# Reordering PE's small solve products in the RWKV-7 heads of a two-layer kernel

## The chip, the cores and the metric

The kernel runs on one core of a Trainium2 chip. The metric is the device time of one execution in microseconds (us), the median of the runs shown. Five engines run side by side and meet only at semaphores: TensorE (PE, with its weight loads as PEld), VectorE (DVE), ScalarE (ACT), GpSimd (POOL) and SyncE (SP, which here only starts DMAs).

## The reference

Two layers run one after the other on 256 tokens of width 2048. The first is a gated mixer with a feed-forward part, the second a hybrid layer with banded attention, an RWKV-7 recurrence and memory cross attention. The change lies in the second layer, where one head of attention and two heads of the recurrence are computed together:

```python
def rwkv7_scan(r, decay, k, v, a_vec, b_vec):
    def step(state, inp):
        r_t, w_t, k_t, v_t, a_t, b_t = inp
        sa = jnp.einsum('bhij,bhj->bhi', state, a_t)
        state = state * w_t[:, :, None, :] + sa[..., None] * b_t[:, :, None, :] + v_t[..., None] * k_t[:, :, None, :]
        return state, jnp.einsum('bhij,bhj->bhi', state, r_t)
    ...

def hybrid_layer(x, mem, norm_g, w_in, ...):
    h = rms_norm(x, norm_g)
    proj = h @ w_in
    (aq, ak, av, az, br, bk, bv, bz, bwd, bad, cq, cz, ga, gb, gc) = jnp.split(proj, offsets, axis=-1)
    ya = chunked_band_attention(aq, ak, av, a_rel_bias) * jax.nn.silu(az)
    yb = rwkv7_time_mix(br, bk, bv, bwd, bad, ...).astype(x.dtype) * jax.nn.silu(bz)
    ...
    return x + merged @ w_o
```

## The kernel before

All large products run in float32 made of three passes: a weight unit of 512 KB (4 x 128 rows by 256 columns) lands in `raw`, ACT rounds it to `w_hi`, DVE makes the rest `w_lo = raw - w_hi` (L1391), and PE multiplies hi by hi, hi by lo and lo by hi. One unit is 24 matmuls of 128x128 weights by 256 columns. Units go through a ring of four. ACT splits unit k+4 as soon as PE has finished unit k, and DVE follows ACT.

The recurrence runs in chunks of 64 tokens, four chunks, two 64-wide heads at once on the upper and lower 64 partitions. Inside a chunk a triangular system is solved by products of 64x64 matrices. A *burst* here is one or two such products for all four chunks and both heads. The function `corners` interleaves two products so that the four 64x64 corners of the array take turns, which makes 32 matmuls.

`late(units)` is written once for each engine and holds the solve of one pair of heads. It runs eight times: seven times in a loop over `heads` (the 16 projection units of the next pair of heads are mixed in) and once with the first 16 units of another projection. `units(k)` means one thing on each engine: PE multiplies unit k (with a second argument, only one half of it, 12 matmuls), ACT makes `w_hi` and DVE `w_lo` of the unit that follows four later in the ring. Every engine works strictly in the order written, and nothing else sets the order. On PE the bursts that matter here are called so in what follows:

- **A**: `No*Q` and `Q*No`, then `Q*At` and `Q*AkV` (64 matmuls)
- **B**: `b2*b1` and `b1*b2`, whose results ACT copies to `N` and `Nt`
- **C**: `N*F` and `Nt*N`, then **T**: three transposes of the softmax weights `prb` (L742)
- **D**: `b3*F` (16 matmuls); DVE adds it to `F`
- **E**: `Y*F` and `F*Kt`, whose results ACT copies to `b2` and `b1`
- after that `state(0)`, `output(0)`, `solve(1)`, `state(1)` and so on: the walk from chunk to chunk, between half units. DVE carries the state `S` and the term `SA` in it (`state`, `solved`).

The order on PE is: unit 3, A, first half of unit 4, B, second half of unit 4, C, T, unit 5, D, unit 6, E, first half of unit 7, `state(0)`. On ACT, `keep(name, bank)` copies a product out of PSUM and tells PE. On DVE, `prepare()` after `units(5)` is `keys_of`, nine operations for the keys of the next pair of heads, and it stands ahead of the first update of `S`. `step` and `to_pe` on DVE both mark an operation done; only `to_pe` is counted by PE's `from_dve()`.

Of the kernel before, what the change touches and what calls it, by code (L numbers as in the profile page):

```python
# [36 lines left out]
HEADS_A = 8  # L37
# [130 lines left out]
def build(nc, a):  # L168
    out_ap = a["out"]
    with ExitStack() as ctx:  # L170
# [91 lines left out]
        bd = {}  # L262
# [123 lines left out]
        def b64(bank):  # L386
            return banks[bank][:, 0:NCH * CHUNK].rearrange("p (c t) -> p c t", c=NCH)
# [35 lines left out]
        def _(pe):  # L423
            n = Counts(pe)
# [71 lines left out]
            for q, (tab, src) in enumerate(((0, f_sum), (1, f_bwd))):  # L496
                for f in range(2):
                    for c in range(2):
# [3 lines left out]
                        for k in range(2):  # L502
                            m = mm(banks[b][:, 0:384], dft[:, tab, k, f * P:(f + 1) * P],
                                   src[:, k, c * 384:(c + 1) * 384], k == 0, k == 1)
# [6 lines left out]
            for c in range(2):  # L511
                for half in range(2):
                    b = 3 + 2 * c + half
                    for j in range(3):
                        m = pe.transpose(banks[b][:, j * P:(j + 1) * P], z1[:, 3 * half + j, c * P:(c + 1) * P],
                                         con_("ident"))
# [4 lines left out]
            for i, (f, c) in enumerate(((0, 0), (0, 1), (1, 0), (1, 1))):  # L521
                if i >= 2:
                    from_dve()
                for part in range(2):
                    b = 3 + 2 * (i % 2) + part
                    for k in range(2):
                        m = mm(banks[b][:, 0:384], dft[:, part, k, f * P:(f + 1) * P],
                               zt[:, k, c * 384:(c + 1) * 384], k == 0, k == 1)
# [3 lines left out]
            for j in range(HY):  # L532
                o = banks[3 + j // 2][:, (j % 2) * T:(j % 2 + 1) * T]
                for i, (src, tab, k) in enumerate(((k_re, 2, 0), (k_re, 2, 1), (k_im, 3, 0), (k_im, 3, 1))):
                    m = mm(o, src[:, k, j * P:(j + 1) * P], dft[:, tab, k, :], i == 0, i == 3)
# [4 lines left out]
            for j in range(HY):  # L540
                m = mm(banks[6][:, 0:T], con_("ones"), gv[:, j, :], j == 0, j == HY - 1)
# [3 lines left out]
            for j in range(HY):  # L545
                m = mm(banks[7][:, 0:T], con_("ones"), gsq[:, j, :], j == 0, j == HY - 1)
# [3 lines left out]
            for e in range(HY):  # L550
                for c in range(2):
                    i = 2 * c + e % 2
                    m = pe.transpose(banks[3 + e // 2][:, i * P:(i + 1) * P], gv[:, e, c * P:(c + 1) * P],
                                     con_("ident"))
# [5 lines left out]
            for e in range(HY):  # L560
                for c in range(2):
                    o = banks[3 + e // 2][:, (e % 2) * T + c * P:(e % 2) * T + (c + 1) * P]
                    m = mm(o, gvt[:, c, e * P:(e + 1) * P], ws[:, e, :])
# [3 lines left out]
            for g in range(4):  # L567
                m = mm(banks[6 + g // 2][:, (g % 2) * T:(g % 2 + 1) * T], pw[:, g, :], pool_d[:, g, :])
# [16 lines left out]
            for half in range(2):  # L585
# [5 lines left out]
                for q in range(4):  # L591
# [5 lines left out]
                    for u in range(11):  # L597
# [6 lines left out]
                        for kk in range(2):  # L604
                            for t in range(4):
# [5 lines left out]
                                m = mm(o, wl, rh, False, u == 10 and kk == 1 and t % 2 == 1)  # L611
# [7 lines left out]
            def product(out, lhs, rhs):  # L619

                return lambda hs, c: mm(out[hs, c, :], lhs(hs, c), rhs(hs, c))
# [7 lines left out]
            def corners(*products):  # L629

                n_, last = len(products), [None] * len(products)
                for j in range(n_):
                    turns = [(j, 0), ((j + 1) % n_, 1)]
                    for c in range(NCH):
                        for i, h in (turns if j == 0 else turns[::-1]):
                            last[i] = products[i](HALVES[h], c)
                return last
# [37 lines left out]
            def late(units):  # L675
# [3 lines left out]
                m = {name: of(t) for name, t in bd.items()}  # L679
# [3 lines left out]
                p, q = corners(product(b4(3), m["b"], both), product(b4(5), m["k"], both))  # L683
                p.then_inc(psum_for_dve, 1)
                q.then_inc(psum_for_dve, 1)
                p, q = corners(product(b64(4), a_, m["b"]), product(b64(2), v_, eye))
# [8 lines left out]
                p, q = corners(product(b64(3), m["Nt"], m["N"]), product(b64(4), m["N"], m["Nt"]))  # L695
# [4 lines left out]
                p, q, r = corners(product(b64(5), m["Kt"], m["Vt"]), product(b64(6), a_, eye), product(b64(2), m["b"], eye))  # L700
# [5 lines left out]
                p, q = corners(product(b64(3), m["b1"], m["Q"]), product(b64(4), m["b2"], m["b1"]))  # L706
# [9 lines left out]
                p, q = corners(product(b64(3), m["b3"], m["Q"]), product(b64(5), m["k"], eye))  # L716
# [5 lines left out]
                p, q = corners(product(b64(3), m["No"], m["Q"]), product(b64(4), m["Q"], m["No"]))  # L722
                p.then_inc(psum_for_dve, 1)
                q.then_inc(psum_for_act, 1)
                p, q = corners(product(b64(5), m["Q"], m["At"]), product(b64(6), m["Q"], m["AkV"]))
                p.then_inc(psum_for_act, 1)
                q.then_inc(psum_for_act, 1)
                units(4, 0)
                from_dve()
                from_act(1)  # L730
                p, q = corners(product(b64(3), m["b2"], m["b1"]), product(b64(4), m["b1"], m["b2"]))
                p.then_inc(psum_for_act, 1)
                q.then_inc(psum_for_act, 1)
                units(4, 1)
                from_act(2)
                from_act(2)
                p, q = corners(product(b64(3), m["N"], m["F"]), product(b64(4), m["Nt"], m["N"]))
# [3 lines left out]
                for i, o in enumerate((0, P, 2 * P)):  # L741
                    t = pe.transpose(banks[7][:, i * P:(i + 1) * P], prb[:, o:o + P], ident)  # L742
                t.then_inc(psum_for_act, 1)
                units(5)
                from_act(1)
                from_dve()
                for c in range(2):
# [6 lines left out]
                        d = 2 - 2 * h + c  # L754
                        t = mm(b64((4, 3)[h])[hs, d, :], bd["b3"][hs, d, :], bd["F"][hs, d, :])
                t.then_inc(psum_for_dve, 1)
                units(6)
                from_dve()
                p, q = corners(product(b64(5), m["Y"], m["F"]), product(b64(6), m["F"], m["Kt"]))
                p.then_inc(psum_for_act, 1)  # L760
                q.then_inc(psum_for_act, 1)
                units(7, 0)
                from_act(3)

# [111 lines left out]
            for j in range(4):  # L876
# [6 lines left out]
                else:  # L883
                    pe.wait_ge(bank_read[(j - 1) % 2], n.now(("fill", (j - 1) % 2)))
                    for c in range(2):
                        for s in range(2):
                            m = pe.transpose(banks[6][:, (2 * c + s) * P:(2 * c + s + 1) * P],
                                             cpair[:, s, c * P:(c + 1) * P], ident)
# [70 lines left out]
        def _(act):  # L959
# [227 lines left out]
            def keep(name, bank):  # L1187

                psum()
                to_pe(copy(flat(bd[name]), banks[bank][:, 0:NCH * CHUNK]))  # L1190
# [42 lines left out]
            def late(units):  # L1233
                keep("Vt", 2)
                psum()
                to_pe(copy(flat(av_t), banks[7][:, 0:T]))
                units(0)
                keep("b1", 3)
                keep("b2", 4)
                keep("At", 6)  # L1240
                keep("AkV", 5)
                keep("Bt", 2)
                keep("b3", 4)
                units(1)
                keep("Kk", 5)
                from_dve()
                act.activation(prb[:, 0:P], prb[:, 0:P], ACT.Exp, bias=stat[:, 2:3], accum_out=stat[:, 4:5])
                to_dve(act.activation(prb[:, P:3 * P], prb[:, P:3 * P], ACT.Exp, bias=stat[:, 3:4],
                                      accum_out=stat[:, 5:6]))
                units(2)  # L1250
                keep("b1", 4)
                keep("Y", 5)
                keep("Kt", 6)
                units(3)
                keep("N", 3)
                keep("Nt", 4)
                keep("b3", 4)
                psum()
                to_pe(copy(prt[:, :], banks[7][:, 0:3 * P]))
                units(4)  # L1260
                units(5)
                keep("b2", 5)
                keep("b1", 6)
                for k in range(6, 10):
                    units(k)
                from_dve()
                psum()
                copy(small["o"][HALVES[0], :], banks[OUT[0]][HALVES[0], 0:T])
                to_pe(copy(small["o"][HALVES[1], :], banks[OUT[1]][HALVES[1], 0:T]))
                units(10)  # L1270
                psum()
                to_pe(act.activation(small["gsq"][:, :], banks[4][:, 0:T], ACT.Square))
                units(11)
                psum()
                to_dve(act.activation(small["groot"][:, :], banks[6][:, 0:T], ACT.Sqrt, bias=con_("eps_gn"),
                                      scale=1.0 / 64))
                for k in range(12, 16):
                    units(k)
# [104 lines left out]
        def _(dve):  # L1383
# [23 lines left out]
            def step(ins):  # L1407
                ins.then_inc(dve_step, 1)
                n.next("step")
# [5 lines left out]
            def to_pe(ins):  # L1415
                ins.then_inc(dve_for_pe, 1)
                n.next("to_pe")
# [18 lines left out]
            def tt(out, x_, y_, op):  # L1436
                return dve.tensor_tensor(out, x_, y_, op)  # L1437
# [457 lines left out]
            def late(units, g, prepare=None):  # L1895
# [38 lines left out]
                to_pe(tt(bd["Q"][:, :, :], bd["Q"][:, :, :], b64(3), ALU.add))  # L1934
                units(2)
                psum()
                step(dve.tensor_copy(bd["b2"][:, :, :], b64(3)))
                to_pe(tt(bd["F"][:, :, :], b64(3), ident4, ALU.add))
                from_act()
                step(dve.reciprocal(stat[:, 6:8], stat[:, 4:6]))  # L1940
# [4 lines left out]
                settle_pe()  # L1945
                psum()
                to_pe(tt(bd["F"][:, :, :], bd["F"][:, :, :], b64(3), ALU.add))
                units(4)
                settle_pe()
                psum()  # L1950
                step(tt(bd["F"][:, 0:2, :], bd["F"][:, 0:2, :], b64(3)[:, 0:2, :], ALU.add))
                to_pe(tt(bd["F"][:, 2:4, :], bd["F"][:, 2:4, :], b64(4)[:, 2:4, :], ALU.add))
                units(5)
                if prepare:
                    prepare()
# [57 lines left out]
            for k in range(16):  # L2013
# [9 lines left out]
                    prefix(k - 5)  # L2023
                if k == 11:
                    to_act(dve.memset(ep4[:, :, 0:1], 1.0))
            with n.loop(HEADS_A - 1, {"unit": 16, "psum": 16, "act": 7, "step": 47, "to_pe": 16, "to_act": 3,
                                      ("fill", 0): 2, ("fill", 1): 2, "bias": 1, "keys": 1, "sums": 1}) as i:
                late(lambda k: heads(k, i + 1), i, lambda: keys_of(i + 1))
            late(queries, HEADS_A - 1)
# [222 lines left out]
```

## Time and profile before

| | |
|---|---|
| Runs | 2412.42, 2415.3, 2416.1 us; median 2415.3 us |
| Profiled execution | 2410.3 us, span 2408.6 us |
| PE busy | 2350.2 us (98%), 21920 matmuls |
| DVE busy | 1508.9 us (63%) |
| ACT busy | 1102.8 us (46%) |
| Mean granted TensorE clock | 0.993 |

The span runs from the first to the last instruction, and 1.7 us lie around it. Matmuls are pipelined and their ends are modelled, so the next one starts before the last has ended: on PE it is the distance between two starts that counts, not the duration.

### The profile page before, as it was taken

The numbers are of one execution on the slowest core, as the hardware profiler recorded it, in microseconds if no ns is written. First come the engines' busy times: TensorE is split into PE (matmuls) and PEld (weight loads), VectorE is DVE, ScalarE is ACT, GpSimd is POOL, SyncE is SP. The second block draws the span as 40 slices with busy tenths as digits, with TensorE's granted clock in tenths as the row PEclk, the third lists the DMA queues.
The fourth block names the chain that finished last, engine by engine and source line by source line (L and its number), as shares of the span: only waits on it lengthen the run. The fifth ranks groups of instructions, "written<-read, shape, count | busy, mean of one in ns | idle before, by whom it ended". The sixth has DMA issues, their size and how long they took to land.

```text
span 2408.6 us, 54358 instructions
## 1 busy us (share of the span) xinstructions
PE 2350.2 (98%) x21920; PEld 2293.3 (95%) x21920; DVE 1508.9 (63%) x2072; ACT 1102.8 (46%) x1455; POOL 12.8 (1%) x27
## 2 busy tenths in 40 slices
PE   6999999999999999997999999999999999999999
PEld 6898999999999999996899999999989999999999
DVE  7556776666546766666866666676576555555554
ACT  5343445555434555434444444444465444444442
POOL 0000000000000000000000000000000000000000
PEclk9999999999999999998999999999999999999999
DMA  6453555555555555554343333333445365555654
GB/s 232 145 185 111 175 184 188 186 187 188 189 187 189 187 188 186 182 183 149 129 134 120 127 119 134 127 127 124 169 147 175 117 203 189 188 189 187 190 189 160
DMA packets 110235, 401.34 MB, mean 167 GB/s; under 512 B 12378, under 2 KB 12405, under 8 KB 109952
## 3 DMA queue, kind: packets, MB, share of 16 engines
q1 hardware_dynamic: 108000, 390.91, 48.9%
q0 software_dynamic: 2080, 8.06, 1.0%
q8 instruction: 136, 2.23, 0.4%
q14 instruction: 19, 0.16, 0.0%
HBM read 396.81 MB, written 2.10 MB: 166 GB/s over the span
## 4 chain that ended last, share of the span: by engine, by line
PE 95%; DVE 3%; ACT 1%; issue 0%; DMA 0%; SPq 0%; DVEq 0%; ACTq 0%
PE bank L428 94%; DVE scratch L1440 1%; DVE w_lo L1391 1%; ACT w_hi L967 0%; DVE h_lo L1437 0%; DMA x<-in_xT 0%; DVE cum L1437 0%; PE bank L742 0%; DVE ping L1437 0%; DVE root L1479 0%; DVE acc L1437 0%; PE bank L691 0%; DVE sq L1437 0%; DVE x L1437 0%; DVE croot L2034 0%
## 5 line engine op out<-in xcount | busy, mean ns | idle before, releaser
L1391 DVE TENSOR_TENSOR w_lo<-raw,w_hi 128x1024 fp32r<-128x1024 f32 x736 | 896.4, 1224 | 707.9 <-ACT w_hi L967 703.4
L967 ACT ACTIVATE w_hi<-raw 128x1024 fp32r<-128x1024 f32 x736 | 779.0, 1060 | 959.8 <-PE bank L428 947.5
L428 PE MATMUL bank<-h_hi,w_hi 128*128 128x256 f32 x4016 | 1148.6, 286 | 20.0 <-DVE h_lo L1437 8.5
L428 PE MATMUL bank<-h_lo,w_hi 128*128 128x256 f32 x4016 | 1125.0, 280 | 0.0
L428 PE MATMUL bank<-h_hi,w_lo 128*128 128x256 f32 x4016 | 1123.4, 280 | 0.0
L428 PEld LDWEIGHTS bank<-h_hi,w_hi 128*128 128x128 f32 x4016 | 758.4, 189 | 35.0 <-issue 12.7
L428 PEld LDWEIGHTS bank<-h_lo,w_hi 128*128 128x128 f32 x4016 | 758.8, 189 | 3.2 <-issue 2.2
L428 PEld LDWEIGHTS bank<-h_hi,w_lo 128*128 128x128 f32 x4016 | 758.3, 189 | 0.0
L428 PE MATMUL bank<-m_hi,w_hi 128*128 128x256 f32 x704 | 196.5, 279 | 0.0
L428 PE MATMUL bank<-m_lo,w_hi 128*128 128x256 f32 x704 | 196.5, 279 | 0.0
L428 PE MATMUL bank<-m_hi,w_lo 128*128 128x256 f32 x704 | 196.5, 279 | 0.0
L428 PEld LDWEIGHTS bank<-m_hi,w_hi 128*128 128x128 f32 x704 | 132.3, 188 | 0.0
L428 PEld LDWEIGHTS bank<-m_lo,w_hi 128*128 128x128 f32 x704 | 132.3, 188 | 0.0
L428 PEld LDWEIGHTS bank<-m_hi,w_lo 128*128 128x128 f32 x704 | 132.3, 188 | 0.0
L428 PE MATMUL bank<-ya_hi,w_hi 128*128 128x256 f32 x384 | 107.2, 279 | 0.0
L428 PE MATMUL bank<-ya_lo,w_hi 128*128 128x256 f32 x384 | 107.2, 279 | 0.0
L428 PE MATMUL bank<-ya_hi,w_lo 128*128 128x256 f32 x384 | 107.2, 279 | 0.0
L1440 DVE SCALAR_TENSOR_TENSOR conv_o<-scaled_up,par,conv_o 128x255 f32<-128x255 f32 x176 | 77.3, 481 | 6.2 <-DVE conv_o L1440 5.9
L428 PE MATMUL bank<-mh_hi,w_hi 128*128 128x256 f32 x256 | 74.5, 291 | 5.4 <-DVE mh_lo L1437 3.4
L428 PEld LDWEIGHTS bank<-ya_hi,w_hi 128*128 128x128 f32 x384 | 72.2, 188 | 0.0
L428 PEld LDWEIGHTS bank<-ya_lo,w_hi 128*128 128x128 f32 x384 | 72.2, 188 | 0.0
L428 PEld LDWEIGHTS bank<-ya_hi,w_lo 128*128 128x128 f32 x384 | 72.2, 188 | 0.0
(404 smaller groups left out, 2714.1 us busy)
## 6 DMA issues: line engine op xcount, KB each, us to landing
raw<-in_units SPq DMA_DIRECT2D x736, 512.0 KB, 3.3
x<-in_xT SPq DMA_DIRECT2D x4, 512.0 KB, 5.9
memx<-in_memT POOLq DMA_DIRECT2D x4, 512.0 KB, 7.5
out_y<-obuf SPq DMA_DIRECT2D x8, 256.0 KB, 4.5
bias_t<-in_bias POOLq DMA_DIRECT2D x8, 192.0 KB, 3.1
dft<-in_dft POOLq DMA_DIRECT2D x1, 1024.0 KB, 8.4
decay<-in_decay POOLq DMA_DIRECT2D x1, 768.0 KB, 6.5
inv<-in_inv POOLq DMA_DIRECT2D x1, 512.0 KB, 3.9
```

The costliest lines, as they stand in the source:

```text
L428: return pe.matmul(out, lhsT, rhs, start=start, stop=stop, skip_group_check=True)
L967: return act.activation(out, in_, ACT.Copy, scale=scale)
L1391: dve.tensor_tensor(w_lo[slot][:, :, :], raw[slot][:, :, :], w_hi[slot][:, :, :].bitcast(F32), ALU.subtract).then_inc(split_done, 1)
L1440: return dve.scalar_tensor_tensor(out, x_, s, y_, op0, op1)
```

## The change

Two places of PE's order change. The first half of unit 4 no longer stands between A and B, and all of unit 4 stands behind B. Unit 5 no longer stands between T and D; it stands between D and E, and unit 6 moves behind E. B writes its first product to bank 2 in place of bank 3, since DVE may still be reading bank 3. The DVE copy of `b2` is now announced to PE on its own, so that B needn't wait for `F` as well; C waits for `F`. ACT and DVE follow in the order of their copies, adds and splits.

```diff
@@ PE, late
                 q.then_inc(psum_for_act, 1)
-                units(4, 0)
                 from_dve()
                 from_act(1)
-                p, q = corners(product(b64(3), m["b2"], m["b1"]), product(b64(4), m["b1"], m["b2"]))
+                p, q = corners(product(b64(2), m["b2"], m["b1"]), product(b64(4), m["b1"], m["b2"]))
                 p.then_inc(psum_for_act, 1)
                 q.then_inc(psum_for_act, 1)
-                units(4, 1)
+                units(4)
+                from_dve()
                 from_act(2)
                 from_act(2)
...
                 t.then_inc(psum_for_act, 1)
-                units(5)
                 from_act(1)
                 from_dve()
...
                 t.then_inc(psum_for_dve, 1)
-                units(6)
+                units(5)
                 from_dve()
                 p, q = corners(product(b64(5), m["Y"], m["F"]), product(b64(6), m["F"], m["Kt"]))
                 p.then_inc(psum_for_act, 1)
                 q.then_inc(psum_for_act, 1)
+                units(6)
                 units(7, 0)
@@ ACT, late
                 keep("Kt", 6)
+                keep("N", 2)
+                keep("Nt", 4)
                 units(3)
-                keep("N", 3)
-                keep("Nt", 4)
                 keep("b3", 4)
                 psum()
                 to_pe(copy(prt[:, :], banks[7][:, 0:3 * P]))
                 units(4)
-                units(5)
                 keep("b2", 5)
                 keep("b1", 6)
-                for k in range(6, 10):
+                for k in range(5, 10):
                     units(k)
@@ DVE, late
-                step(dve.tensor_copy(bd["b2"][:, :, :], b64(3)))
+                to_pe(dve.tensor_copy(bd["b2"][:, :, :], b64(3)))
...
                 to_pe(tt(bd["F"][:, :, :], bd["F"][:, :, :], b64(3), ALU.add))
-                units(4)
                 settle_pe()
                 psum()
                 step(tt(bd["F"][:, 0:2, :], bd["F"][:, 0:2, :], b64(3)[:, 0:2, :], ALU.add))
                 to_pe(tt(bd["F"][:, 2:4, :], bd["F"][:, 2:4, :], b64(4)[:, 2:4, :], ALU.add))
+                units(4)
                 units(5)
```

On PE, at C, T and D, before (`m_b_121` is `b3`, `L742` the transposes; the rows left out are matmuls of the same unit):

```order
L428 MATMUL bank<-m_N,m_Nt 64x64
L742 MATMUL bank<-con,prb 128x128 x3
L428 MATMUL bank<-h_hi,w_hi 128x256
...
L428 MATMUL bank<-h_hi,w_lo 128x256
L428 MATMUL bank<-m_F,m_b_121 64x64 x8
L428 MATMUL bank<-h_hi,w_hi 128x256
```

and with the change:

```order
L428 MATMUL bank<-m_N,m_Nt 64x64
L742 MATMUL bank<-con,prb 128x128 x3
L428 MATMUL bank<-m_F,m_b_121 64x64 x8
L428 MATMUL bank<-h_hi,w_hi 128x256
L428 MATMUL bank<-h_lo,w_hi 128x256
```

The whole of unit 5 has left the place between the transposes and D. The matmuls on either side of it are the same.

On ACT, the copies of E's results, `b2` (`m_b_116`) and `b1` (`m_b_115`), and the splits around them:

```order
 L975 REGISTER_ALU
 L967 ACTIVATE w_hi<-raw 128x1024
-L975 REGISTER_ALU
-L967 ACTIVATE w_hi<-raw 128x1024
 L986 REGISTER_ALU
 L967 ACTIVATE m_b_116<-bank 128x256
 L986 REGISTER_ALU
 L967 ACTIVATE m_b_115<-bank 128x256
+L975 REGISTER_ALU
+L967 ACTIVATE w_hi<-raw 128x1024
```

One split, that of `units(5)`, has moved from ahead of the two copies to behind them.

On DVE, from the add of C's product to the keys of the next heads, before:

```order
L1437 TENSOR_TENSOR m_F<-m_F,bank 128x256
L1390 REGISTER_ALU
L1391 TENSOR_TENSOR w_lo<-raw,w_hi 128x1024
L1420 REGISTER_ALU
L1402 REGISTER_ALU
L1437 TENSOR_TENSOR m_F<-m_F,bank 128x128 x2
L1390 REGISTER_ALU
L1391 TENSOR_TENSOR w_lo<-raw,w_hi 128x1024
L1434 ISA
L1437 TENSOR_TENSOR s_t_128<-s_pr 128x256
```

and with the change, whose lines have numbers lower by one there:

```order
L1436 TENSOR_TENSOR m_F<-m_F,bank 128x256
L1419 REGISTER_ALU
L1401 REGISTER_ALU
L1436 TENSOR_TENSOR m_F<-m_F,bank 128x128 x2
L1389 REGISTER_ALU
L1390 TENSOR_TENSOR w_lo<-raw,w_hi 128x1024
L1389 REGISTER_ALU
L1390 TENSOR_TENSOR w_lo<-raw,w_hi 128x1024
L1433 ISA
L1436 TENSOR_TENSOR s_t_128<-s_pr 128x256
```

The two parts of the add to `F` stand together, and both splits stand behind them, still ahead of the keys.

## Rows read from the trace of the kernel before

**Rows 1.** The page: busy time of the engines, and the chain that ended last

```profile
PE 2350.2 (98%) x21920; PEld 2293.3 (95%) x21920; DVE 1508.9 (63%) x2072; ACT 1102.8 (46%) x1455; POOL 12.8 (1%) x27
PE 95%; DVE 3%; ACT 1%; issue 0%; DMA 0%; SPq 0%; DVEq 0%; ACTq 0%
```

**Rows 2.** Window of one pair of heads: length, then each engine's busy time, clock, DMA

```profile
1281.77:1350.65 68.88, 68.88 (x874) 64.99 (x873) 47.22 (x88) 31.92 (x56) 0.55 (x1) 1.00 0.39 126
```

**Rows 3.** Timeline of PE (start, duration, what): a joined place, then A, unit 4, B

```profile
1202.65 0.22 PE L428 MATMUL bank<-m_N,m_Nt 64*64 64x64 f32 x1
1202.70 0.22 PE L428 MATMUL bank<-m_Vt,m_Kt 64*64 64x64 f32 x1
...
1214.75 0.22 PE L428 MATMUL bank<-m_At,m_Q 64*64 64x64 f32 x1
1214.90 0.38 PE L428 MATMUL bank<-h_hi,w_hi 128*128 128x256 f32 x1
1215.12 0.28 PE L428 MATMUL bank<-h_lo,w_hi 128*128 128x256 f32 x1
...
1216.30 0.28 PE L428 MATMUL bank<-h_hi,w_lo 128*128 128x256 f32 x1
1216.51 1.15 PE L428 MATMUL bank<-m_b,m_b 64*64 64x64 f32 x32
```

**Rows 4.** Timeline of DVE and ACT behind A: the copies that B needs

```profile
1214.08 0.43 DVE L1937 COPY m_b<-bank 128x256 f32<-128x256 f32 x1 [0.59 <-PE bank L428]
1214.12 0.39 ACT L967 ACTIVATE m_b<-bank 128x256 f32<-128x256 f32 x1 [1.89 <-PE bank L428]
```

**Rows 5.** Timeline of PE: T, D, E, `solve(1)`, `state(1)`

```profile
1220.28 0.55 PE L742 MATMUL bank<-con,prb 128*128 128x128 f32 x3
...
1223.56 0.68 PE L428 MATMUL bank<-m_F,m_b 64*64 64x64 f32 x16
...
1227.17 0.27 PE L428 MATMUL bank<-m_F,m_Y 64*64 64x64 f32 x1
...
1232.74 0.33 PE L428 MATMUL bank<-S,m_b 64*64 64x64 f32 x4
...
1234.62 0.33 PE L428 MATMUL bank<-SA,m_Bt 64*64 64x64 f32 x4
```

**Rows 6.** Timeline of DVE: adds to F, splits, keys, first states

```profile
1220.38 0.42 DVE L1437 TENSOR_TENSOR m_F<-m_F,bank 128x256 f32<-128x256 f32 x1 [2.51 <-PE bank L428]
...
1224.29 0.48 DVE L1437 TENSOR_TENSOR m_F<-m_F,bank 128x128 f32<-128x128 f32 x2 [0.73 <-PE bank L428]
1224.76 1.23 DVE L1391 TENSOR_TENSOR w_lo<-raw,w_hi 128x1024 fp32r<-128x1024 f32 x1
...
1229.44 0.48 DVE L1440 SCALAR_TENSOR_TENSOR s_rk<-s_r,par,s_k 128x256 f32<-128x256 f32 x1
1230.35 0.60 DVE L1443 TENSOR_SCALAR S<-bank,s_ep 64x64 f32<-64x64 f32 x2 [0.42 <-PE bank L428]
1231.64 0.43 DVE L1440 SCALAR_TENSOR_TENSOR yall<-bank,az 128x256 f32 x1 [0.69 <-PE bank L428]
1231.98 1.22 DVE L1391 TENSOR_TENSOR w_lo<-raw,w_hi 128x1024 fp32r<-128x1024 f32 x1
...
1233.28 0.47 DVE L1437 TENSOR_TENSOR SA<-bank,m_b 64x64 f32<-64x64 f32 x2
```

**Rows 7.** Timeline of ACT: the split of `units(5)`, E's copies, the split behind

```profile
1223.66 1.06 ACT L967 ACTIVATE w_hi<-raw 128x1024 fp32r<-128x1024 f32 x1 [1.36 <-PE bank L428]
1228.36 0.66 ACT L967 ACTIVATE m_b<-bank 128x256 f32<-128x256 f32 x2 [3.63 <-PE bank L428]
1228.90 1.06 ACT L967 ACTIVATE w_hi<-raw 128x1024 fp32r<-128x1024 f32 x1
```

**Rows 8.** Timeline of DVE and PEld: a unit that PE waited for

```profile
1251.53 1.22 DVE L1391 TENSOR_TENSOR w_lo<-raw,w_hi 128x1024 fp32r<-128x1024 f32 x1
...
1252.83 0.19 PEld L428 LDWEIGHTS bank<-h_hi,w_hi 128*128 128x128 f32 x1 [0.24 <-DVE w_lo L1391]
```

More of the change, by code:

```diff
@@ L2025, in _ @@
                     to_act(dve.memset(ep4[:, :, 0:1], 1.0))
-            with n.loop(HEADS_A - 1, {"unit": 16, "psum": 16, "act": 7, "step": 47, "to_pe": 16, "to_act": 3,
+            with n.loop(HEADS_A - 1, {"unit": 16, "psum": 16, "act": 7, "step": 46, "to_pe": 17, "to_act": 3,
                                       ("fill", 0): 2, ("fill", 1): 2, "bias": 1, "keys": 1, "sums": 1}) as i:
```

## The prediction

> **What bounds the kernel now.** I read the page first. PE is busy 98% of the span, and 95% of the chain that ended last is PE, 3% DVE, 1% ACT [rows 1]. So a PE matmul removed or a wait on PE counts in full, and work of DVE and ACT counts only where PE waits for it. I then took the window of one pair of heads, since the change lies in `late` alone: it is 68.88 us long, PE has no idle time in it, the granted clock is 1.00, and DVE is busy 47 us of it [rows 2]. The change moves nothing in the other three quarters of the span. "PE busy" is not "PE at its peak", because the ends of matmuls are modelled. So I went on to the timelines and read distances between starts: of PE around A and B [rows 3] and from T to `state(1)` [rows 5], and of DVE and ACT in the same stretch [rows 4, 6, 7]. They show two things. PE loses some tenths of a microsecond at each change between 128x128 weight units and 64x64 bursts. And DVE, idle on average, is without a gap to speak of between the last add to `F` and the first update of `S`. All other heads repeat this pattern, seven with the keys of the next heads in DVE's queue and the last one without them.
>
> **No work goes.** The same matmuls, copies, adds, splits and DMAs are issued; only order changes. What can change is what PE loses between them.
>
> **Join of A and B.** Inside a unit, ten steps take 1216.30 - 1215.12 = 1.18 us, so one matmul takes 0.118 us [rows 3]. From the last matmul of A to the first of B pass 1216.51 - 1214.75 = 1.76 us [rows 3]. Of these, 12 x 0.118 = 1.42 us are the half unit, which is moved and must be paid elsewhere; 0.34 us are lost to going over and back. Where two bursts already follow one another, with waits between them, the distance is 1202.70 - 1202.65 = 0.05 us [rows 3]. So the join gives 0.34 - 0.05 = 0.29 us per pair of heads. It needs B's operands in time. DVE's copy of `b2` ends at 1214.08 + 0.43 = 1214.51, ACT's copy of `b1` at 1214.12 + 0.39 = 1214.51 [rows 4]. The best row for the time from DVE's end to PE's start is the unit that PE waited for: DVE ended at 1251.53 + 1.22 = 1252.75, and PE's load began at 1252.83, 0.08 us later [rows 8]. So B may start at 1214.59, and A keeps PE until 1214.80. The second half of A hides the copies with 0.2 us to spare. If that cover were short, B would lose at most the spare and some tenths more: the bounds are 0.05 and 0.34 us gained.
>
> **Join of T and D.** From T to D pass 1223.56 - 1220.28 = 3.28 us [rows 5]. A unit is 24 x 0.118 = 2.83 us, so 0.45 us are lost on the way. With the unit gone, D needs `F`, and the add that makes it begins only when C's product has ended: it runs from 1220.38 to 1220.80 [rows 6], that is to 0.52 us behind the start of T. ACT's copy of `b3` runs beside it. With 0.08 us for the semaphore, D starts at T + 0.60. The three transposes can't cover that. So in place of 0.45 us, 0.60 us are lost: the join costs 0.15 us per pair of heads. Bounds: if the add were no hindrance, D would follow the transposes at about T + 0.3, 0.15 us gained; if ACT's copy of `b3` ends half its length later than the add (the copies are 0.39 and 0.43 us long [rows 4]), 0.35 us are lost.
>
> A rule on that place. The rows show 0.34 us lost where the array goes from 64x64 tiles to 128x128 and back [rows 3]. The Trainium skill, in TensorEngine Tiling (Array Packing), section Key Properties, says that changing the tiling mode drains TensorE. By that rule the second join takes away no change of mode at all, since the transposes have 128x128 weights like the unit did and D still follows them in 64x64, so it would give nothing even without the wait; the first takes away two. By the rows alone one might count 0.45 us for the second join, which would make the whole change worth 8 x (0.29 + 0.45) = 5.9 us without waits; by the rule it would be 8 x 0.29 = 2.3 us.
>
> **What is moved behind them: a new wait in `solve(1)` and `state(1)`.** This is the term that decides. Times here are counted from the start of D.
> - PE. E follows at 1227.17 - 1223.56 = 3.61 with one unit between, before and after alike [rows 5]. `solve(1)` stands at 1232.74 - 1223.56 = 9.18 and `state(1)` at 11.06 [rows 5]. With the change one more unit lies in between (unit 5, that stood ahead of D), so PE could be there at 9.18 + 2.83 = 12.01 and 13.89.
> - ACT. The split of `units(5)` starts 0.10 us behind D now [rows 7]. With the change it is queued behind the two copies of E's results. These start 1228.36 - 1227.17 = 1.19 us behind E's start, so at 4.80, and the next split starts 0.54 us later [rows 7], at 5.34; it takes 1.06 us and ends at 6.40.
> - DVE. Its `w_lo` follows at once, at 6.40 where it now starts at 1.20 [rows 6]: 5.2 us later, while PE's part that must cover it grew by only 2.83 us. Behind it in DVE's queue stand the nine operations of the keys and then `S`. From the start of that `w_lo` to the end of the last key operation pass 1229.92 - 1224.76 = 5.16 us [rows 6]. So the keys end at 11.56, `S` (0.60 us) at 12.16, and PE may start `solve(1)` at 12.24: 0.23 us late. Then `yall` from 12.16, the next `w_lo` 0.34 us later at 12.50, `SA` 1.30 us after that from 13.80 to 14.27 [rows 6]. PE may start `state(1)` at 14.35, 0.46 us behind the 13.89 that it could keep. The 0.23 us are contained in this.
>
> Before, DVE waited 0.42 us for PE at `S` [rows 6], so this wait is new. After `state(1)` the next `S` has slack again, and nothing that starts there depends on the lost time. Bounds per pair of heads: 0, if the key operations, some of which overlap by 0.1 us, run on into `S` and the rest sooner than I lay them end to end; and 0.8 us, if DVE's operations follow one another without the overlap that the row of `yall` shows: it ends at 1232.07, and the next starts 0.09 us earlier [rows 6]. Four such places from `S` to `SA` make 0.46 + 0.36 = 0.82 us. I take 0.46, since the distances that it is made of are those of the rows.
>
> The last pair of heads has no keys in the queue and so no such wait. Unit 4's own split on DVE, now behind the second add to `F`, and the units moved behind B cost nothing: PE reads these splits three units later, over 8 us.
>
> **Sum.** Seven pairs of heads: -0.29 + 0.15 + 0.46 = +0.32 us each, together +2.2; the last: -0.14. In all +2.1 us on the profiled execution's 2410.3 us (span 2408.6), so 2412.4 us there. The three runs shown lie above that execution, with a mean of 2414.6 and a median of 2415.3 us; since their spread of 3.7 us is larger than the effect I put the sum on the mean: 2416.7, say 2417 us. A difference of under 0.2% (4.8 us) can't be told from no change here.
>
> **Rivals.**
> - *No new wait.* The DVE chain runs faster than laid out or the slack is larger. For it: the chain is within 0.5 us of fitting, and I added up thirteen rows. Against it: `w_lo` moves by 5.2 us against 2.83 us of added cover. Then only the joins count: 8 x (-0.29 + 0.15) = -1.1 us, 2413.5 us.
> - *Both joins pay in full.* D's operands come sooner and no wait arises. Time: 8 x (-0.29 - 0.15) = -3.5 us, 2411 us; with the whole 0.45 us for the second join it would be -5.9 us, 2409 us. Against it: the add to `F` can't begin before C's product has ended, and that is seen in its row [rows 6].
> - *Clearly slower.* The same wait, but larger. DVE's operations behind the keys follow one another without overlap, `state(1)` is 0.82 us late, and D loses 0.35 in place of 0.15 us. That makes 7 x (-0.29 + 0.35 + 0.82) + 0.06 = +6.2 us, 2421 us. It decides where the late `S` and `SA` cost more than about 0.8 us per pair of heads with D's 0.15 us as forecast (7 x (0.83 - 0.14) = 4.8 us). For it: DVE would have no idle time left there to make good what it lost. Against it: the overlap is in the row of `yall` [rows 6].
> - *The change doesn't do what it says*: T and D are no real join (above). That is contained in my forecast as the 0.15 us lost.
>
> **How the numbers follow.** My forecast 0.55; no new wait 0.22; clearly slower 0.15; both joins in full 0.08. All four lie close together against a spread of 3.7 us between runs. The range is 2412 to 2422 us: down to the case without a new wait less the runs' spread, up to the slow case with the same. Faster by over 0.2%: most of the last case, 0.07. Slower by over 0.2%: most of the slow case and a piece of my own with unlucky runs, 0.18. Within 0.2%: 0.75.
>
> **What the changed profile would show.** The first matmul of B 0.05 to 0.1 us behind the last of A. D 0.6 us behind T, with its wait put down to DVE or ACT. The `w_lo` of `units(5)` some 6.4 us behind D, and no idle time of DVE ahead of the first `S`. PE's `solve(1)` 12.2 and `state(1)` 14.35 us behind D in seven of eight. A window of one pair of heads of 69.2 us in place of 68.88. I am wrong if `state(1)` comes at 13.9, if D follows T at 0.3, or if that window is under 68.7 or over 69.8 us.

## The result and the profile after

| | before | with the change |
|---|---|---|
| Median of 15 runs | 2415.2 us (2410.1 to 2417.9) | 2418.3 us (2413.7 to 2426.2) |
| Ratio, 95% interval | | 1.0021 [1.0012, 1.0030] |
| Profiled execution, span | 2408.6 us | 2421.8 us |
| From T to T of the next pair of heads, seven times | 482.1 us | 486.5 us |

The ratio of 1.0021 says that the change costs about 5 us of 2415, 3 to 7 us by its interval; the medians lie 3.1 us apart, the means 5.3. The profiled execution shows 13.2 us more span, and most of that is not the change: 6.8 us are there before the first T, 4.4 us arise in the seven pairs of heads, and 2.0 us behind the last T (last section). On the page the busy shares hardly differ, 97% for PE in place of 98 and 62% for DVE in place of 63. The chain that ended last does, with more of it on DVE (95% and 3% before, [rows 1]):

```profile
PE 92%; DVE 5%; issue 1%; ACT 1%; DMA 0%; DVEq 0%; SPq 0%; ACTq 0%
```

Where PE waits for DVE, the waits that end on PE's weight loads in the solve tell, here of the kernel with the change (who waited for whom, total us, times, longest; a row for `w_lo`, 1.7 us as before, is left out):

```profile
PEld bank L428 <- DVE SA L1436: 4.9, 7, 0.7
PEld bank L428 <- issue: 4.5, 15, 0.5
PEld bank L428 <- ACT m_b L967: 2.8, 8, 0.4
PEld bank L428 <- DVE S L1442: 2.1, 7, 0.4
```

Before there was no row of `SA`, `S` or `m_b`. Seven times PE waits for `S` and for `SA`, in the seven pairs of heads that have the keys of the next in DVE's queue; eight times it waits for `b3` (`m_b`).

The timeline of PE with the change answers to [rows 3] and [rows 5]:

```profile
1221.88 0.22 PE L428 MATMUL bank<-m_At,m_Q 64*64 64x64 f32 x1
1221.93 1.10 PE L428 MATMUL bank<-m_b,m_b 64*64 64x64 f32 x32
...
1226.91 0.22 PE L428 MATMUL bank<-m_F,m_N 64*64 64x64 f32 x1
1227.06 0.55 PE L742 MATMUL bank<-con,prb 128*128 128x128 f32 x3
1227.74 0.68 PE L428 MATMUL bank<-m_F,m_b 64*64 64x64 f32 x16
...
1231.37 0.27 PE L428 MATMUL bank<-m_F,m_Y 64*64 64x64 f32 x1
...
1240.00 0.33 PE L428 MATMUL bank<-S,m_b 64*64 64x64 f32 x4 [0.17 <-DVE S L1442]
...
1242.43 0.33 PE L428 MATMUL bank<-SA,m_Bt 64*64 64x64 f32 x4 [0.50 <-DVE SA L1436]
```

B follows A at 0.05 us. D stands 0.68 us behind T. E follows D at 3.63 us, as before. `solve(1)` stands at 12.26 and `state(1)` at 14.69 us behind D, where PE, by the forecast's sum, could have been at 12.01 and 13.89.

DVE and ACT in the same stretch, answering to [rows 6] and [rows 7]:

```profile
1227.17 0.42 DVE L1436 TENSOR_TENSOR m_F<-m_F,bank 128x256 f32<-128x256 f32 x1 [1.24 <-PE bank L428]
1228.47 0.49 DVE L1436 TENSOR_TENSOR m_F<-m_F,bank 128x128 f32<-128x128 f32 x2 [0.88 <-PE bank L428]
...
1234.19 1.23 DVE L1390 TENSOR_TENSOR w_lo<-raw,w_hi 128x1024 fp32r<-128x1024 f32 x1 [3.85 <-ACT w_hi L967]
...
1238.87 0.48 DVE L1439 SCALAR_TENSOR_TENSOR s_rk<-s_r,par,s_k 128x256 f32<-128x256 f32 x1
1239.34 0.60 DVE L1442 TENSOR_SCALAR S<-bank,s_ep 64x64 f32<-64x64 f32 x2
1240.27 0.42 DVE L1439 SCALAR_TENSOR_TENSOR yall<-bank,az 128x256 f32 x1 [0.33 <-DVE S L1442]
1240.61 1.22 DVE L1390 TENSOR_TENSOR w_lo<-raw,w_hi 128x1024 fp32r<-128x1024 f32 x1
...
1241.90 0.47 DVE L1436 TENSOR_TENSOR SA<-bank,m_b 64x64 f32<-64x64 f32 x2
```

```profile
1227.21 0.38 ACT L967 ACTIVATE m_b<-bank 128x256 f32<-128x256 f32 x1 [1.99 <-PE bank L428]
...
1232.56 0.66 ACT L967 ACTIVATE m_b<-bank 128x256 f32<-128x256 f32 x2 [3.47 <-PE bank L428]
1233.10 1.06 ACT L967 ACTIVATE w_hi<-raw 128x1024 fp32r<-128x1024 f32 x1
```

DVE stands idle for 3.85 us waiting for ACT's split of `units(5)`, which is behind E's copies. From there to `SA` it never waits for another engine. Two gaps of 0.18 and 0.16 us among the keys stand there before as well; the one that counts is that `yall` starts 0.93 us behind `S`, after 0.33 us in which it waits for `S` itself.

The last pair of heads is a control inside the same profile. It has the same order, D comes just as late (0.74 us behind T) and so does the `w_lo` (6.43 us behind D), but no keys stand in DVE's queue.

```profile
1714.32 0.68 PE L428 MATMUL bank<-m_F,m_b 64*64 64x64 f32 x16 [0.20 <-DVE m_F L1436]
...
1728.16 0.33 PE L428 MATMUL bank<-SA,m_Bt 64*64 64x64 f32 x4
```

There `state(1)` stands 13.84 us behind D, without a wait.

### The profile page after: what moved, and what is told of

Same layout as the page of the kernel before. It is cut to its first block, busy times and chain, and to the rows that moved or that the text cites. A ratio compares the mean times of both kernels' runs of the same rounds, so it can differ in the third digit from the quotient of the medians.

```text
span 2421.8 us, 54358 instructions
## 1 busy us (share of the span) xinstructions
PE 2358.0 (97%) x21920; PEld 2300.7 (95%) x21920; DVE 1508.4 (62%) x2072; ACT 1099.9 (45%) x1455; POOL 12.8 (1%) x27
## 4 chain that ended last, share of the span: by engine, by line
PE 92%; DVE 5%; issue 1%; ACT 1%; DMA 0%; DVEq 0%; SPq 0%; ACTq 0%
PE bank L428 91%; DVE w_lo L1390 1%; DVE scratch L1439 1%; ACT w_hi L967 1%; DVE h_lo L1436 0%; DVE s_k L1439 0%; DMA x<-in_xT 0%; DVE cum L1436 0%; DVE S L1442 0%; DVE ping L1436 0%; DVE s_t L1436 0%; DVE root L1478 0%; PE bank L742 0%; DVE acc L1436 0%; PE bank L691 0%
```

## The experiments

In the profiles the stretch over seven pairs of heads, from the first T to the last, repeats to about 0.1 us in the three kernels that were profiled more than once, while the whole varies by several us. So each experiment is read from both. The lines below show the first and last start of the transposes (duration min/median/max in ns, then the two starts in us). The last start is that of the third transpose of the last T, about 0.2 us behind its first; the table counts from the first transpose of a T to the first of another, from the timelines. Before and the change:

```profile
L742 PE MATMUL bank<-con,prb x24: 272/273/330, 1220.3 to 1702.6; 128*128 128x128 f32 x24
```

```profile
L742 PE MATMUL bank<-con,prb x24: 272/273/330, 1227.1 to 1713.9; 128*128 128x128 f32 x24
```

For the first join alone, for the second alone, and for the change with the split turned back:

```profile
L742 PE MATMUL bank<-con,prb x24: 272/273/330, 1219.6 to 1699.4; 128*128 128x128 f32 x24
```

```profile
L742 PE MATMUL bank<-con,prb x24: 272/273/330, 1219.4 to 1708.6; 128*128 128x128 f32 x24
```

```profile
L742 PE MATMUL bank<-con,prb x24: 272/273/331, 1220.5 to 1701.9; 128*128 128x128 f32 x24
```

| kernel | seven pairs of heads, us | one, against before | median, us | ratio to before [95%] |
|---|---|---|---|---|
| before | 482.07 | | 2415.1 / 2416.1 / 2415.6 | |
| the change | 486.52, 486.39, 486.42 | +0.64, +0.62, +0.62 | 2418.3 / 2417.7 / 2420.8 | 1.0021 [1.0012, 1.0030]; 1.0011 [1.0002, 1.0020]; 1.0013 [0.9997, 1.0029] |
| first join alone | 479.50, 479.56 | -0.37, -0.36 | 2413.8 / 2414.5 | 0.9990 [0.9979, 1.0000]; 0.9994 [0.9985, 1.0003] |
| second join alone | 488.90 | +0.98 | 2426.1, six runs | 1.0039 [1.0024, 1.0055] |
| split turned back | 481.12 | -0.14 | 2412.8 | 0.9995 [0.9985, 1.0006] |
| late settle | 484.48, 484.47 | +0.34 | 2420.3 / 2420.2 | 1.0021 [1.0012, 1.0030]; 1.0010 [0.9994, 1.0026] |
| six transposes | 487.20 | +0.73 | 2417.0, one run | |
| D ahead of T | 488.36 | +0.90 | 2423.5, one run | |

The first time of the change is that of the result above, beside 2415.2 us of before. The three medians of before are those of the three batches in which the experiments ran: the change (second figure), both joins alone and the split turned back ran in the first batch; the late settle, the first join again, the six transposes and D ahead of T in the second; the change and the late settle once more in the third.

**The change again.** The kernel unaltered, in the first batch with three others and in the third:

> The changed kernel again, beside the kernels with one part of it. Both theories: 1.0021 times the kernel before (+5 us), the window from one pair of heads to the next 69.5 us against 68.87 us.

> The changed kernel a third time, beside the one with the late wait of yall. Expected: ratio 1.0010 to 1.0021 as in the two measurements so far, a pair of heads 69.5 us.

Measured 1.0011 and 1.0013. All three intervals overlap between 1.0012 and 1.0020. The stretch gives +4.3 to +4.5 us over seven pairs; that is 0.0018 of the whole.

**The first join alone.** On PE A, B, unit 4, C, T, unit 5, D, unit 6, E; ACT's two copies (`N`, `Nt`) ahead of the split of `units(3)`, as in the change. ACT's split of `units(5)` and DVE's of `units(4)` stand where they stood before.

```diff
-                units(4, 0)
-                p, q = corners(product(b64(3), m["b2"], m["b1"]), product(b64(4), m["b1"], m["b2"]))
+                p, q = corners(product(b64(2), m["b2"], m["b1"]), product(b64(4), m["b1"], m["b2"]))
-                units(4, 1)
+                units(4)
+                from_dve()
```

> Only the join of A and B. My theory: it is the useful part; B follows A at 0.05 us, no wait appears, each pair of heads is 0.35 us shorter (0.30 us of 1.76 us between A and B, 0.05 us within B), 68.5 us in place of 68.87, and the time falls by 8 x 0.35 = 2.8 us, ratio 0.9988. Rival: the loss comes from this part, since two copies on ACT now stand ahead of the split of unit 3's slot and bank 2 is used; then the ratio is above 1.001 and DVE's chain up to S is late here too.

Measured 0.9990, and 0.37 us less per pair. B follows A at 0.05 us here too, and no wait for `S`, `SA` or `b3` appears. This refutes the rival. In the second batch:

> The join of A and B alone once more, now as the version to keep. Both earlier measurements and theory: 68.5 us per pair of heads, 8 x 0.37 = 3.0 us under before, ratio 0.9988 of before; the interval should touch or exclude 1.000. If the ratio is above 1.0005, the gain seen in the profile is given back elsewhere.

Measured 0.9994 [0.9985, 1.0003], with 479.56 us: the sign holds, but the interval doesn't exclude 1.

**The second join alone.** All edits of the change but those above.

```diff
-                units(5)      # PE, behind T
...
-                units(6)
+                units(5)      # behind D
...
+                units(6)      # behind E
```

> Only the join of T and D, with units 5 and 6 moved as in the change. My theory: all of the loss is here. D 0.68 us behind T in place of 0.45 us beyond a unit (+0.23 us), state(1) 14.7 us behind D in place of 13.89 (+0.80 us): +1.03 us in seven pairs of heads and +0.23 us in the last, +7.4 us, ratio 1.0031. Rival (the loss comes from the first join): ratio at or below 1.000.

Measured 1.0039, +0.98 us per pair. The two parts add: -0.36 + 0.98 = +0.62 us, and the change has +0.62 to +0.64. The whole loss is in the second join.

**The split turned back.** The changed kernel, with one line on ACT at its old place:

```diff
                 units(4)
+                units(5)
                 keep("b2", 5)
                 keep("b1", 6)
-                for k in range(5, 10):
+                for k in range(6, 10):
```

> The changed kernel with one thing turned back: ACT makes the high half of units(5) ahead of the copies of E's results, not behind them. My theory: the wait at solve(1) and state(1) stems from that split's place. The split then starts as PE ends unit 5 (3.6 us behind D) and ends before E's product is done, so the copies are not late; w_lo starts at 4.8 in place of 6.45 us behind D, and the wait of 0.80 us is gone: 0.12 us per pair of heads better than before, ratio 0.9996 against before, about 5 us under the changed kernel. Rival: the wait comes from the mere number of operations in DVE's queue behind D or from D's own lateness, and stays: ratio 1.002 as the changed kernel.

Measured 0.9995 and -0.14 us per pair, 0.76 us less than the change. In its timelines (ACT, then DVE, then PE) the split is 1.06 us that end just as E's product does:

```profile
1224.90 1.06 ACT L967 ACTIVATE w_hi<-raw 128x1024 fp32r<-128x1024 f32 x1 [2.37 <-PE bank L428]
1225.98 0.66 ACT L967 ACTIVATE m_b<-bank 128x256 f32<-128x256 f32 x2
```

```profile
1225.99 1.23 DVE L1391 TENSOR_TENSOR w_lo<-raw,w_hi 128x1024 fp32r<-128x1024 f32 x1 [2.20 <-ACT w_hi L967]
```

```profile
1221.18 0.68 PE L428 MATMUL bank<-m_F,m_b 64*64 64x64 f32 x16
...
1235.02 0.33 PE L428 MATMUL bank<-SA,m_Bt 64*64 64x64 f32 x4
```

`w_lo` starts 4.81 us behind D, not 6.45, and `state(1)` stands at 13.84 without a wait, as in the last pair of heads. The number of operations in DVE's queue is the same, so it is the place of the split on ACT that makes the wait.

**The late settle.** `settle_pe()` makes DVE wait until its own operations that PE is told of have ended. In the changed kernel it is moved behind `yall` and the split of `units(6)`, so `yall` no longer waits for `S`:

```diff
-                settle_pe()
                 psum()
                 dve.wait_ge(bank_read[1], n.now(("fill", 1)))
                 step(stt(y_tile(g), banks[6][:, 0:T], 0.5, az[:, :], ALU.mult, ALU.mult))
                 units(6)
+                settle_pe()
```

> The changed kernel; on DVE the wait for the end of the first update of S stands behind yall and the split of units(6), not ahead of yall. My theory: my sum forgot this wait; in the changed profile yall starts 0.93 us behind S where I laid 0.60, and 0.33 us of the 0.80 us at state(1) are due to it. With it moved, state(1) comes 14.35 us behind D in place of 14.69, and a pair of heads takes 69.2 us in place of 69.5: 7 x 0.33 = 2.3 us less than the changed kernel, ratio to before about 1.0005. Rival: the 0.33 us are the price of yall's own read of PSUM; then nothing moves and the pair of heads stays at 69.5.

The mechanism came out as expected: `yall` starts 0.63 us behind `S` (1234.39 and 1235.02), `state(1)` at 14.40 us behind D, and a pair of heads takes 484.48 / 7 = 69.21 us. The time did not: 1.0021 where 1.0005 was expected, and 1.0005 lies outside its interval. So I ran it again beside the change:

> The late wait of yall again. In the profile the pair of heads fell to 69.21 us as expected, the time did not follow (1.0021). If that was scatter of single programs, the ratio now lies 0.001 (2 us) under that of the changed kernel in the same batch. Rival: something outside the solve takes the 2 us back; then it is not under the changed kernel's ratio, and the stretch between the last transposes of the solve and the cross attention is longer than there, as it was by 1.4 us in the one profile.

Now it is 1.0010 beside 1.0013: the median is 0.6 us lower, and 2 us can neither be confirmed nor excluded. The stretch behind the solve, from the last T to the first copy of `cpt`, is longer, as the rival said: 161.0 and 160.8 us in this kernel, 159.5, 159.6 and 159.8 in the change. The trace shows where. Some 100 us behind the last T, PE has waited 3.4 us for `mh_lo`, and the matmuls behind that wait start 0.21 us apart in place of 0.117: the lower of the clock's two levels, 1.2 in place of 2.4 GHz. In this kernel it stays low for longer. A window of 17 us around the place, first in the change (its second profile), then in this kernel (its first): PE's busy time and matmuls come first behind the length, the mean granted clock behind the five engines.

```profile
1801.00:1818.00 17.00, 13.56 (x103) 13.36 (x102) 11.50 (x16) 10.10 (x12) 0.00 (x0) 0.90 0.60 189
```

```profile
1801.00:1818.00 17.00, 13.56 (x91) 13.36 (x92) 11.92 (x16) 8.79 (x10) 0.00 (x0) 0.80 0.55 176
```

But the rest of the kernel doesn't take the 2 us back. Some 44 us further on, where PE has waited 1.7 and 0.7 us for ACT, 32 matmuls run at a mean granted clock of 0.81 and take 8.5 us in all three profiles of the change; in both of this kernel they run at 1.00 and take 6.8. The same two profiles:

```profile
L428 PE MATMUL bank<-cpt,mvt x32: 379/379/634, 1909.2 to 1917.7; 128*128 128x256 f32 x32
```

```profile
L428 PE MATMUL bank<-cpt,mvt x32: 379/379/483, 1911.3 to 1918.1; 128*128 128x256 f32 x32
```

From the last T to the end it is 712.6 and 712.4 us in this kernel, 708.2, 712.9 and 708.3 in the change, and the 4.7 us that the change's second profile has more arise behind these matmuls (last section). So the rival isn't borne out: the profiles lose 1.3 us in one place and win 1.7 in another. No edit touches either place. The split turned back and the six transposes have the longer stretch too (161.0 us each), and before and the six transposes have the 6.8 us. What makes the clock rise sooner or later there is open.

**Six transposes.** The changed kernel with T made twice over the same place:

```diff
-                for i, o in enumerate((0, P, 2 * P)):
+                for i, o in enumerate((0, P, 2 * P) * 2):
+                    i = i % 3
```

> The changed kernel with the three transposes T made twice, the second time over the same place. If D, 0.68 us behind T, waits for F and b3, the three extra transposes (0.10 us each) fill the wait: D stays within 0.05 us of 0.68 us behind the first transpose, and the pair of heads at 69.5 us. Rival: what D loses is the change from 128x128 to 64x64 behind T; then D moves to 0.98 us and the pair of heads takes 69.8 us.

```profile
1220.22 0.88 PE L743 MATMUL bank<-con,prb 128*128 128x128 f32 x6
1221.03 0.68 PE L428 MATMUL bank<-m_F,m_b 64*64 64x64 f32 x16
```

D stands 0.81 us behind the first transpose, between the two expectations of 0.68 and 0.98, and the wait for `m_b` is gone from the list. So of the 0.33 us of added transposes 0.20 filled a wait; the other 0.13 delay D, and a pair of heads takes 0.11 us more than in the change. It follows, as an estimate, that without the wait D would stand at about 0.48 us behind T (0.81 - 0.33), while before it stood 0.45 us and a unit behind it. The join saves nothing even where its operands come in time.

**D ahead of T.** C, D, T, unit 5:

```diff
-                for i, o in enumerate((0, P, 2 * P)): ...     # behind C
...
                 t.then_inc(psum_for_dve, 1)                   # end of D
+                for i, o in enumerate((0, P, 2 * P)): ...
                 units(5)
```

> The changed kernel with D ahead of T: C, D, T, unit 5. D then follows C without a change of tile size between them. If D waits for F and b3 alone, it starts as long behind C's last matmul as now (0.83 us) less a tenth, and the three transposes no longer lie in the wait but cost their 0.30 us: the pair of heads takes 69.7 us. Rival (the change of tile size behind T is what holds D): D follows C within 0.3 us and the pair of heads takes 69.3 us or less.

```profile
1219.92 0.22 PE L428 MATMUL bank<-m_F,m_N 64*64 64x64 f32 x1
1220.74 0.68 PE L428 MATMUL bank<-m_F,m_b 64*64 64x64 f32 x16 [0.60 <-ACT m_b L967]
```

```profile
1220.17 0.42 DVE L1436 TENSOR_TENSOR m_F<-m_F,bank 128x256 f32<-128x256 f32 x1 [1.23 <-PE bank L428]
```

D starts 0.82 us behind C's last matmul, as in the change (0.83), though no tile size changes in between, and the pair of heads takes 69.8 us. The rival falls: D is held by its operands. In both, D starts 0.15 us behind the end of DVE's add (1220.59 here).

## Why the prediction was right, point by point

The direction, the place and the size of the loss came out as laid down: 2418.3 us lie in the range near 2417, and the ratio of 1.0021 lies on the border between "within 0.2%" and "slower", which got chances of 0.75 and 0.18. The sum of +2.1 us was too small: the seven pairs of heads alone lost 4.3 to 4.5 us. All three terms were off in size. So that the median lies only 1.3 us from the forecast is in part luck: with the terms as measured, the forecast's base of 2414.6 us would have given about 2419.

- *First join.* Forecast -0.29 us, measured -0.36 to -0.37 (first join alone). The distance from A to B fell from 1.76 to 0.05 us as forecast. I left out that B itself is shorter behind a 64x64 burst: from its first matmul to the next unit 1.03 us (1221.93 to 1222.96) in place of 1.08.
- *Second join.* Forecast +0.15 us, measured +0.23 (0.68 - 0.45 us). The term that was too small is the 0.08 us from DVE's end to PE's start. I read it from [rows 8], where the trace names `w_lo` as releaser. That was no wait for `w_lo`: PE had just been given two matmuls of 512 columns,

```profile
1252.40 1.02 PE L428 MATMUL bank<-qr,con 128*128 128x512 f32 x2
```

  and the next matmul starts 0.46 us behind the first of them (1252.86), which is 4 x 0.118 us for 4 x 256 columns: PE lost no time there. In the changed profile the loads of `solve(1)` and `state(1)` follow the ends of `S` and `SA` at 0.05 us. D, which waits for DVE and ACT both, has its load 0.12 and its first matmul 0.15 us after the add and the copy, which both end at 1227.59. Why it takes longer there is open. The 0.45 us was also misread as a loss: three transposes alone take 0.33 us of it (0.88 - 0.55 us for three more), so only 0.12 us of it is lost, and "both joins pay in full" promised too much.
- *New wait.* Forecast 0.46 us, measured 0.80 against the forecast's 13.89, and 0.85 against the 13.84 us at which `state(1)` stands without a wait; turning the split back takes 0.76 us off a pair of heads. The chain was right up to `S`: `w_lo` at 6.45 us behind D (forecast 6.40), the keys' end at 11.61 (11.56), the end of `S` at 12.20 (12.16), `solve(1)` at 12.26 (12.24). The step that was wrong is "then `yall` from 12.16": it started at 12.53. DVE settles `S` ahead of `yall`, a line that I had before me and laid no time for. In [rows 6] this can't be seen, because `yall` waited longer for PE. The late settle moved `state(1)` by 0.29 us, most of the 0.34 that the forecast lacked. The upper bound of 0.8 us was met, but not for its reason: `yall` and the split behind it still overlap by 0.08 us, and no wait of DVE's own stood in that bound.
- *Tile sizes.* By the rule of the Trainium skill that I weighed (TensorEngine Tiling (Array Packing), Key Properties: a change of tiling mode drains TensorE), the second join would give nothing and the first all. The six transposes agree: less the 0.33 us of the transposes, 0.15 us would be lost without the wait where 0.12 us were.
- *Cause.* In the split turned back D is as late as in the change (0.67 us behind T), only `w_lo` comes sooner, and `state(1)` stands at 13.84 us. In the last pair of heads D and `w_lo` are both late, only the keys are missing, and it stands at 13.84 us too. So the wait needs the late `w_lo` and the keys behind it, and D's lateness doesn't make it.
- *The mean as base.* Before measured 2415.2 us over 15 runs; from the median of the three runs shown the same sum would have given 2417.4 us, nothing that can be told apart.

A version faster than both: the first join alone, 0.9990 and 0.9994 of before. Both intervals reach 1, so the gain in the whole isn't shown beyond doubt; both profiles show 2.5 to 2.6 us less in the seven pairs.

## What to carry to other kernels

Work that is moved away between two dependent pieces was cover for all engines, not just the one whose order one looks at: write down for each queue what stands behind the moved item, and lay the chain to the next meeting point. Here one 1 us split, put behind two copies, came 5.2 us later for 2.8 us of new cover, and turning that one line back took the wait away. When a chain is laid out from rows, each wait in the code between two of its steps needs a duration, also where the trace hides it under a longer one. And bursts are worth joining where the array's tile size stays the same and the operands are ready, not where other work with another tile size lies between.

## What the runs showed of the hardware that I had not expected

Executions of these kernels differ by several us in parts that none of the edits touches, and in steps. Two of them are the places where the granted clock is low for longer or shorter, told under the late settle (1.3 and 1.7 us). The other two are stretches in which PE runs without a gap at a granted clock of 1.00 and yet at one of two paces.

The first lies ahead of the solve. DVE's first operation that makes `lt` from `lx`, early in the second layer, starts at 1136 to 1138 us in nine of the twelve profiles (before among them) and at 1143 to 1144 us in three. One program shows both: the change has 1143.2, 1136.5 and 1143.7, the late settle 1137.8 and 1143.9. From 300 to 1014 us, where most of the difference arises, PE has 0.4 us of waits in the profile of before and 0.4 us in that of the change. But it starts 6113 matmuls in that window in the profile of before, and 6061 in that of the change, one every 0.1168 and every 0.1178 us:

```profile
300.00:1014.00 714.00, 713.56 (x6113) 713.26 (x6112) 464.62 (x612) 349.20 (x442) 0.00 (x0) 1.00 0.56 187
```

```profile
300.00:1014.00 714.00, 713.57 (x6061) 713.26 (x6060) 461.57 (x609) 345.35 (x440) 0.00 (x0) 1.00 0.55 186
```

The second lies at the end. From the last matmul of `cpt` and `mvt` to the end of the span it is 496.3 to 496.4 us in four profiles (before, the change's first and third, the six transposes), with 429 to 431 matmuls in 50 us, and 501.0 to 501.1 us in the other eight, with 425 to 427. The profile of before is on the short side in both stretches and at `cpt` and `mvt`, and it is the shortest of the twelve by 3 us, though the first join alone has the shorter solve.

In the window from 300 to 1014 us the three passes take 281, 280 and 278 ns on the mean in the three longer executions, and 279 each in the others. What sets the rhythm is open. For reading such profiles it means that a difference of spans between two executions is no measure of a change of 0.2%; the distance between two marks around the edit, which repeats to about 0.1 us here, is.
